# Layer 1 of a two-layer decoder: who splits the output weights into high and low halves

## The reference

```python
q, k, v = jnp.split(u @ w_qkv + b_qkv, [...], axis=-1)      # 16 query heads, 2 key/value heads, 64 wide
...
scores = jnp.einsum('bnqhgd,bnkhd->bnhgqk', qb, kk) * (SWA_HEAD_DIM ** -0.5)
scores = jnp.where(valid, scores, -jnp.inf)                 # window of 128 tokens
m = jnp.maximum(jnp.max(scores, axis=-1), sink)
p = jnp.exp(scores - m[..., None])
denom = jnp.sum(p, axis=-1) + jnp.exp(sink - m)
o = jnp.einsum('bnhgqk,bnkhd->bnhgqd', p, vv) / denom[..., None]
return o @ w_o + b_o                                        # w_o is 1024 x 1024
```

## Time and profile before

| what | value |
|---|---|
| median of 3 runs | 2073.36 us (2072.98 to 2074.16) |
| the profiled execution, its time | 2069.8 us |
| its span, first to last instruction | 2068.1 us |
| PE busy over the span | 2005.8 us (97%) |
| DVE, ACT, POOL busy | 1576.0, 1338.0, 277.5 us (76%, 65%, 13%) |
| the eight w_o_high on ACT | start from 1227.6 to 1248.8 us |

### The profile page before, as it was taken

How to read it: one execution, slowest core, us unless ns; L and a number is a source line. 1 busy time by engine, 2 the same in 40 slices (tenths; PEclk the granted TensorE clock), 3 DMA queues, 4 the chain that set the end, 5 groups by cost and what they waited for, 6 DMA issues and landing times. The chain is left out here.

```text
span 2068.1 us, 29817 instructions
## 1 busy us (share of the span) xinstructions
PE 2005.8 (97%) x10448; PEld 1636.6 (79%) x10448; DVE 1576.0 (76%) x1878; ACT 1338.0 (65%) x1818; POOL 277.5 (13%) x345
## 2 busy tenths in 40 slices
PE   7999998998999999999998989999899999999998
PEld 6888876887788888888886866777688888888885
DVE  4561235776888898889888357887898988889886
ACT  5332425663787878887873157664688777878784
POOL 2000000001211111111103422110211111112210
PEclk9999999999999999999999999999999999999999
DMA  4112222124999999999996020013799999999996
GB/s 142 41 58 86 71 75 88 72 75 179 350 384 390 388 389 386 382 376 383 387 358 214 1 78 25 22 62 113 267 390 385 383 385 387 387 387 386 383 356 258
DMA packets 123487, 513.24 MB, mean 248 GB/s; under 512 B 27373, under 2 KB 28490, under 8 KB 89610
## 3 DMA queue, kind: packets, MB, share of 16 engines
q1 hardware_dynamic: 103674, 474.11, 61.0%
q0 software_dynamic: 18576, 33.86, 4.3%
q10 hardware_dynamic: 1152, 4.19, 0.5%
HBM read 495.05 MB, written 50.86 MB: 264 GB/s over the span
## 5 line engine op out<-in xcount | busy, mean ns | idle before, releaser
L517 DVE TENSOR_TENSOR exp_w_lo<-ring_raw,first_w_hi 128x2048 fp32r<-128x2048 f32 x192 | 438.8, 2287 | 32.7 <-ACT first_w_hi L444 32.6
L517 DVE TENSOR_TENSOR exp_w_lo<-ring_raw,exp_w_hi 128x2048 fp32r<-128x2048 f32 x192 | 439.3, 2290 | 27.8 <-ACT exp_w_hi L444 27.7
L444 ACT ACTIVATE exp_w_hi<-ring_raw 128x2048 fp32r<-128x2048 f32 x192 | 367.8, 1918 | 60.4 <-PE exp_up_out L369 32.5
L444 ACT ACTIVATE first_w_hi<-ring_raw 128x2048 fp32r<-128x2048 f32 x188 | 360.5, 1918 | 60.9 <-PE exp_up_out L369 30.1
L314 POOL DMA_INDIRECT y_rows<-exp_y,base_rows_y x63 | 79.0, 1254 | 947.2 <-ACT exp_y L464 934.0
L369 PE MATMUL exp_gate_out<-exp_w_lo,exp_x_hi 128*128 128x512 f32 x512 | 199.8, 390 | 0.0
L369 PE MATMUL exp_y_out<-exp_w_lo,exp_hid_hi 128*128 128x512 f32 x512 | 199.6, 390 | 0.0
L369 PE MATMUL exp_up_out<-exp_w_lo,exp_x_hi 128*128 128x512 f32 x512 | 199.2, 389 | 0.0
L369 PE MATMUL exp_gate_out<-first_w_hi,exp_x_hi 128*128 128x512 f32 x272 | 109.3, 402 | 3.1 <-issue 2.0
L521 DVE TENSOR_TENSOR exp_x_lo<-exp_x_turned,exp_x_hi 128x1024 fp32r<-128x1024 f32 x62 | 75.9, 1224 | 47.6 <-ACT exp_x_hi L448 47.6
L369 PEld LDWEIGHTS exp_up_out<-exp_w_lo,exp_x_hi 128*128 128x128 f32 x512 | 96.1, 188 | 19.8
(11 more groups left out here) (535 smaller groups left out, 4632.2 us busy)
## 6 DMA issues: line engine op xcount, KB each, us to landing
ring_raw<-in_expert_w_gate_dram SPq DMA_DIRECT2D x128, 1024.0 KB, 10.9
ring_raw<-in_expert_w_up_dram SPq DMA_DIRECT2D x128, 1024.0 KB, 11.4
ring_raw<-in_expert_w_down_dram SPq DMA_DIRECT2D x128, 1024.0 KB, 11.3
l0w_raw<-in_ab_w_in_dram SPq DMA_DIRECT2D x48, 256.0 KB, 2.8
finish_y<-y_rows SPq DMA_DIRECT2D x8, 1024.0 KB, 12.7
ring_raw<-in_swa_w_qkv_dram SPq DMA_DIRECT2D x5, 1024.0 KB, 9.4
ring_raw<-y_rows SPq DMA_DIRECT2D x10, 512.0 KB, 4.4
base_h<-in_x_dram ACTq DMA_DIRECT2D x8, 512.0 KB, 6.8
```

Source lines behind the costliest of these rows:

```text
L444: nc.scalar.activation(split[split_slot(unit)][0][:], raw[raw_slot(unit)][:], ACT.Copy).then_inc(hi_ready, 1)
L517: nc.vector.tensor_tensor(lo[:], raw[raw_slot(unit)][:], hi[:].bitcast(F32), ALU.subtract).then_inc(lo_ready[split_slot(unit)], 1)
```

## The change

The high halves of the odd chunks move from ScalarE to GpSimd: there each half of 512 columns is a copy into the reduced format, a drain, and the subtraction as before. GpSimd no longer waits for ScalarE but for the transfer of the chunk. ScalarE keeps the even chunks' high halves, one a group in groups 1 to 4, at the place behind exponents; the one between norms and next_queries goes. The counts that VectorE waits for follow: chunk k is the (k/2 + 5)th high half made.

```diff
-    W_O_HIGH_AT = {1: (0, 1), 2: (2, 3), 3: (4, 5), 4: (6, 7)}
+    W_O_HIGH_AT = {1: 0, 2: 2, 3: 4, 4: 6}
...
-            def odd_low(k):
-                pool.wait_ge(s["w_hi_made"], k + 5)
+            def odd_chunk(k):
+                pool.wait_ge(w_ready[k // 2], 32)
                 for cols in (slice(0, BANK), slice(BANK, 1024)):
+                    g.tensor_copy(w_hi[:, k, cols], w_raw[:, k, cols])
+                    pool.drain()
                     last = g.tensor_tensor(w_lo[:, k, cols], w_raw[:, k, cols], w_hi[:, k, cols].bitcast(F32), ALU.subtract)
                 last.then_inc(s["odd_split"], 1)
-            odd_low(1)
-            odd_low(3)
+            odd_chunk(1)
+            odd_chunk(3)
             rotate(T - 1)
-            odd_low(5)
-            odd_low(7)
+            odd_chunk(5)
+            odd_chunk(7)
...
                 if G < LAST - 1:
                     norms(G + 1)
-                if G in W_O_HIGH_AT:
-                    w_o_high(W_O_HIGH_AT[G][0])
                 if G < LAST - GROUPS:
                     next_queries(G)
...
                 if G in W_O_HIGH_AT:
-                    w_o_high(W_O_HIGH_AT[G][1])
+                    w_o_high(W_O_HIGH_AT[G])
...
             def w_o_low(k):
-                dve.wait_ge(s["w_hi_made"], k + 5)
+                dve.wait_ge(s["w_hi_made"], k // 2 + 5)
```

## The result

The changed kernel is slower: 2078.86 us against 2073.56 us (medians of eight runs each), a ratio of 1.0029 (95% interval 1.0019 to 1.0039), that is +6.0 us (+3.9 to +8.1 us). The ratio is one of means; the medians differ by 5.3 us. Forecast were +8.6 us and 2082.0 us. The profiled execution spans 2075.6 us, 7.5 us more than the one before.

The account below looks back on a forecast made before the run. DVE's own loop was taken as the chain that bounds the stretch. 8.27 - 0.58 - 1.83 + 2.7 = +8.6 us took the median from 2073.4 to 2082.0 us, range 2077.5 to 2086.0 us.

Parts of the forecast that it names:

- The main term: Groups 1 to 4: DVE's even subtraction waits for ACT's conversion, now behind exponents; +8.27 us.
- DVE's wait for copy_own: Group 2: DVE's wait for ACT's copy_own goes, as ACT is then ahead; -0.58 us.
- the signs named: Line 2956 some 2.75 us after 3006, ended by ACT; PE idling 8 us more; experts later; 3004 lengthened in groups 0, 1.
- The prediction's 1265 us: Time near which PE would be full again in the changed profile, after idling some 8 us more.
- rival 1: DVE's idle time ahead of band_probs in groups 5 to 8 returns 5.9 us: +2.7 us, 2076.1 us; chance 0.13.
- GpSimd's terms: DVE's delays by POOL: old ones leave, -1.83 us; new ones come with eight copies of 0.90 us each, +2.7 us.
- seven old delays: DVE delays by POOL from 1233.91 to 1252.57 us, 2.41 us in sum; the first five, 1.83 us, on the chain.
- the two-input rule of the prediction: From the Trainium skill: a GpSimd instruction reading SBUF can shut out a two-SBUF-input VectorE one for its whole length.
- the rate per us of GpSimd work: DVE loses 0.166 us per us of POOL work, 76% on the chain; applied to 21.7 us, +2.7 us.
- ACT as the bound: Rival 2: ACT's four conversions leave, DVE's wait is hidden, 1.4 to 4.2 us won: 2069.2 to 2072.0 us; chance 0.04.
- The clock: Rival 3: PE's gaps in the stretch grow and TensorE's clock falls, 3.4 us: +12.0 us, 2085.4 us; chance 0.06.
- Late odd halves: Rival 4: POOL's chunk 7 comes after PE needs it and PE waits, under 2 us more; chance 0.02.

Follow-up runs that it names:

- run 1: Changed kernel with the even chunks' high halves put back ahead of next_queries, GpSimd's part kept: 2075.10 us, ratio 1.0008 to the kernel before.
- run 2: Kernel before, with only ACT's two conversions of each group in the other order (odd first, even behind exponents): 2081.03 us, ratio 1.0041.
- run 3: Changed kernel with DVE's subtraction of the even chunks one group later (groups 2 to 5): 2073.27 us, ratio 1.0001 to the kernel before.
- run 4: Changed kernel with each of GpSimd's eight copies made twice: 2084.78 us, ratio 1.0057 to the kernel before.
- run 5: Changed kernel without GpSimd's copies and their drains, odd high halves not made: 2082.02 us, ratio 1.0048 to the kernel before.
- run 6: Kernel with doubled GpSimd copies, plus 14 idle transposes on TensorE ahead of weigh in groups 4 and 5: 2082.27 us, ratio 1.0049 to the kernel before.
- run 9: Even high halves ahead of next_queries, all low halves on GpSimd, its instructions cut from 512 to 256 columns: 2073.46 us, ratio 0.9998 to the kernel before.
- run 7: Changed kernel with even high halves ahead of next_queries and all eight low halves on GpSimd: 2073.71 us, ratio 1.0008 to the kernel before.

## Why the prediction was right, and where it was off

**The main term held.** Forecast: 2.75 us from line 3006 to line 2956 in each of four groups, 11.00 - 2.73 = +8.27 us. Measured: 11.06 - 2.73 = +8.33 us. That this wait is the loss is shown by runs 1, 2 and 3 from three sides. The 0.58 us of DVE's wait for copy_own went, as forecast. Of the signs named, the wait and its engine came; line 3004 was lengthened in group 0, but not in group 1, where chunk 3 was done before it.

**It passed to the end, nearly whole.** PE is full from 1259.4 us on, where it was from 1251.4 us before, 8.0 us later. The prediction's 1265 us counts from 1256.9 us, the edge of a window in which PE was full already. PE idles only 3.8 us more in the stretch (11.6 against 7.8 us), as at the lower clock the same matmuls kept it busy 4.1 us longer. The catching up of rival 1 did not come: DVE waits 2.25 us for PE in group 6 of the changed kernel and PE takes no notice. (The four waits of the earlier trace rows are those of groups 6 to 9, not 5 to 8.) Of the 7.88 us 0.6 us came back between the stretch and the experts. The largest gain there is where the clock of the earlier trace rows had fallen: the 24 idle transposes took 5.32 us before and 4.40 us after. PE before, then after:

```profile
1438.45 5.32 PE L2712 MATMUL l_wide<-base_ident 128*128 128x128 f32 x24
...
1446.24 4.40 PE L2714 MATMUL l_wide<-base_ident 128*128 128x128 f32 x24
```

**GpSimd's terms were off, both of them.** I counted seven old delays, 2.41 us. One of them is the pause ahead of line 3013. DVE before:

```profile
1250.55 0.18 DVE L3013 RECIPROCAL l_inv<-l_inv 128x4 f32<-128x4 f32 x1 [0.45 <-issue]
```

It returns as 0.45 us of "issue" at 1258.57 us in the changed kernel, when GpSimd had been idle for over 3 us, so there it was not GpSimd's; and line 3013 reads one operand only, so this one of the seven did not agree with the two-input rule of the prediction. The old delays without it are 2.03 us, of which 1.45 us (not 1.83 us) on the chain. The new ones are 1.86 us, not 2.7 us. The copy is 0.61 us, near the low end (0.53 us), not 0.90 us; the Trainium skill (GPSIMD Engine Reference, Engine selection) with its line rate, 0.43 us by estimate, was the better guide than the row of 1.76 us, though no copy ran that fast. With these sizes the sum is 8.33 - 0.58 - 1.45 + 1.86 = +8.16 us against a stretch of +7.88 us. Most of the 0.3 us is the wait for copy_own again: from line 3013 to line 2998 DVE took 0.77 us in group 2 and 0.23 us in group 4 before, and 0.10 and 0.09 us after, 0.81 us in sum where the term has 0.58 us. The step that failed is the rate per us of GpSimd work: runs 4, 5, 6 and 9 show that the delays do not follow it. That its error stayed small here (+0.41 us net, where -1.83 + 2.7 = +0.9 us was forecast) was luck: twice the copies gave 4.97 us of delays in run 4 and 2.60 us in run 6. A copy does delay DVE (0.26 us at 1224.11 us) and is delayed by it (1.60 us at 1247.32 us). The Trainium skill (SBUF - State Buffer, Who interferes with whom) says that a VectorE instruction with two SBUF inputs contends with a GpSimd instruction that reads SBUF, and that the order of issue decides which of them is blocked. The trace agrees, in both orders.

**The median.** 2082.0 us were forecast, 2078.86 us came. Of the 3.1 us between them, 0.7 us is the stretch (7.88 against 8.6 us) and 0.6 us what came back ahead of the experts. The other 1.8 us is not traced. Executions of one kernel differ by more (2070.07 to 2074.55 us before): the two profiled ones differ by 7.5 us, the medians by 5.3 us, and the ratio says 6.0 us with an interval up to 8.1 us, just under the forecast.

**The rivals.** ACT as the bound would have made the kernel faster. It got slower, and in run 1, where ACT's relief stays, nothing is won. The clock did fall, which I had given 0.06, but not where it costs: ACT and DVE took what PE made late without idle time. In runs 4 and 5 such a fall did cost, 2.7 and 1.4 us. Late odd halves: PE's list shows no such wait.

## What to carry to other kernels

Before moving a conversion between two engines, ask of the half that stays at which place of its engine's list it stands, and what the consumer has done by then: here the second place lay behind a step that waits for the consumer's own last result, and a loop between two engines got a second round trip. An engine that is the fullest of a stretch need not be its bound; look for the one whose late start others wait for. The delays between two engines that shut each other out were set here by when their instructions met, and a term for them needs a range, not a rate.

## What was not expected of the hardware

GpSimd with less work delayed VectorE more, in one profile each: 4.04 us with no copies against 1.86 us with them, and 4.97 us with twice as many. In run 6, again with twice as many, it was 2.60 us. TensorE's granted clock fell to 0.50 (1.2 GHz) for 6 us behind 5 us in which it was busy for 1.88 us, and stayed at 1.00 in the kernel before behind 4 us with 1.93 us busy; such a fall cost 2.7 us in one kernel and nothing in another. A pause of 0.45 us ahead of line 3013 of group 6, put down to "issue", is there in nine of the twelve profiles, with GpSimd at work (before) and idle (changed), and not in runs 3, 7 and 9; its cause stays open.
